# Reordering the vector engine's queue at eleven hand-offs and in the last step of a mixture-of-experts kernel

## The reference

```python
def swiglu(h, wg, wu, wd):
    return (jax.nn.silu(h @ wg) * (h @ wu)) @ wd

def moe_swiglu(h, router, eg, eu, ed):
    b, s, d = h.shape
    t = h.reshape(b * s, d)
    logits = (t @ router).astype(jnp.float32)
    top_v, top_i = lax.top_k(logits, TOP_K)
    top_w = jax.nn.softmax(top_v, axis=-1)
    ...
    out = jnp.zeros((b * s, d), jnp.float32)
    for e in range(N_EXPERTS):
        out = out + combine[:, e:e + 1] * swiglu(t, eg[e], eu[e], ed[e]).astype(jnp.float32)
    return out.astype(h.dtype).reshape(b, s, d)
```

## Time and profile before

| what | value |
|---|---|
| median of 3 runs | 1355.52 us (1355.41 to 1357.62) |
| the profiled execution, its own time | 1355.3 us |
| its span, first to last instruction | 1353.5 us |
| PE busy | 1320.2 us (98%) |
| DVE busy | 1120.3 us (83%) |
| ACT busy | 941.3 us (70%) |
| weight loads in the profile | 423.23 MB on the queue of SP |

### The profile page before, as it was taken

One profiled execution on the slowest core, in us unless ns is written; L12 is line 12 of the kernel. 1 busy time (PEld: TensorE's weight loads), 2 busy tenths in 40 slices (PEclk: granted clock), 3 DMA queues, 4 the chain that ended last, 5 costly groups with the idle time before them and its releaser, 6 DMA issues.

```text
span 1353.5 us, 17501 instructions
## 1 busy us (share of the span) xinstructions
PE 1320.2 (98%) x6684; PEld 1098.8 (81%) x6685; DVE 1120.3 (83%) x1037; ACT 941.3 (70%) x879; POOL 104.2 (8%) x67
## 2 busy tenths in 40 slices
PE   8999999999999999999999999999999999999994
PEld 5898888887898878888888888887888888888873
DVE  5767655556766899999999999999999999999986
ACT  4644444444644778788787887887878787888774
POOL 1140000000231100100001001100000001000020
PEclk9999999999999999999999999999999999999998
DMA  9434655553523799999999999999999999999992
GB/s 354 183 108 161 232 187 186 186 199 113 186 97 138 303 365 378 410 404 420 410 402 421 415 414 403 416 420 375 416 418 404 420 399 410 415 421 419 407 420 92
DMA packets 63029, 437.47 MB, mean 323 GB/s; under 512 B 7231, under 2 KB 7409, under 8 KB 11746
## 3 DMA queue, kind: packets, MB, share of 16 engines
q1 hardware_dynamic: 58896, 423.23, 78.2%
q0 software_dynamic: 3904, 13.06, 2.6%
q10 hardware_dynamic: 146, 0.07, 0.0%
HBM read 430.04 MB, written 6.29 MB: 322 GB/s over the span
## 4 chain that ended last, share of the span: by engine, by line
PE 86%; DVE 8%; ACT 2%; DMA 2%; issue 1%; SPq 0%; DVEq 0%; ACTq 0%
PE ps L2118 34%; PE ps L2142 18%; PE ps L2238 8%; PE ps L1806 4%; DVE w_lo L405 4%; PE ps L2258 4%; PE ps L1821 4%; PE ps L1909 3%; PE ps L2247 2%; PE ps L1783 2%; DMA raw<-in_stream 2%; ACT w_hi L400 1%; PE ps L2134 1%; DVE spare_w L405 1%; PE ps L2178 1%
## 5 line engine op out<-in xcount | busy, mean ns | idle before, releaser
L405 DVE TENSOR_TENSOR w_lo<-raw,w_hi 128x2048 fp32r<-128x2048 f32 x313 | 715.2, 2303 | 125.8 <-ACT w_hi L400 124.8
L400 ACT ACTIVATE w_hi<-raw 128x2048 fp32r<-128x2048 f32 x315 | 600.1, 1917 | 163.6 <-PE ps L2118 67.6
L2118 PE MATMUL ps<-w_hi,xT_hi 128*128 128x512 f32 x564 | 224.3, 398 | 1.8 <-DVE xT_lo L1366 1.3
L2118 PE MATMUL ps<-w_lo,xT_hi 128*128 128x512 f32 x564 | 220.4, 391 | 0.0
L2118 PE MATMUL ps<-w_hi,xT_lo 128*128 128x512 f32 x564 | 219.7, 390 | 0.0
L405 DVE TENSOR_TENSOR spare_w<-raw,spare_w 128x2048 fp32r<-128x2048 f32 x85 | 194.5, 2288 | 10.0 <-ACT spare_w L400 9.5
L400 ACT ACTIVATE spare_w<-raw 128x2048 fp32r<-128x2048 f32 x85 | 163.1, 1918 | 18.7 <-PE ps L2142 16.1
L2118 PEld LDWEIGHTS ps<-w_hi,xT_hi 128*128 128x128 f32 x564 | 106.1, 188 | 23.0 <-DVE xT_lo L1366 1.5
L2118 PEld LDWEIGHTS ps<-w_lo,xT_hi 128*128 128x128 f32 x564 | 105.9, 188 | 22.8
L2118 PEld LDWEIGHTS ps<-w_hi,xT_lo 128*128 128x128 f32 x564 | 106.2, 188 | 20.8
L2142 PE MATMUL ps<-w_hi,aT_hi 128*128 128x512 f32 x288 | 114.1, 396 | 2.6 <-DVE w_lo L405 2.0
(11 more groups left out here) (352 smaller groups left out, 1983.4 us busy)
## 6 DMA issues: line engine op xcount, KB each, us to landing
raw<-in_stream SPq DMA_DIRECT2D x400, 1024.0 KB, 7.9
outs<-work POOLq DMA_DIRECT2D x5, 512.0 KB, 9.2
gain<-in_gains POOLq DMA_DIRECT2D x4, 512.0 KB, 5.3
h<-in_x SPq DMA_DIRECT2D x2, 512.0 KB, 6.7
raw<-in_stream SPq DMA_DIRECT2D x2, 512.0 KB, 6.4
tokens<-big POOLq DMA_DIRECT2D x2, 512.0 KB, 3.3
outs<-work POOLq DMA_DIRECT2D x4, 256.0 KB, 7.6
out<-work SPq DMA_DIRECT2D x4, 256.0 KB, 2.8
```

The source lines that it names most:

```text
L400: nc.scalar.activation(home(n, 0), raw[:, n % RAW, :], ACT.Copy).then_inc(hi_done, 1)
L405: nc.vector.tensor_tensor(home(n, 1), raw[:, n % RAW, :], home(n, 0).bitcast(F32), ALU.subtract).then_inc(lo_done, 1)
L2118: last = nc.tensor.matmul(ps[:, 4 + s, :], (xT_hi, xT_lo)[xp][:, k, x * P:(x + 1) * P], w((n + half), wp, kk * 512, (kk + 1) * 512), start ...
```

## The change

Only DVE's queue is reordered, in its function `step(i)`. Nothing is computed more or less often.

- At the eleven steps of `TURN_AT` the gathered low part stands ahead of `lo_unit(m + 7)` and no longer behind it.
- In step 54 `light_mul` and `light_lo` of the first of the last two light blocks stand ahead of `lo_unit(m + 7)`, the split of the last unit.
- In step 54 `combine(0, 1)` and `combine(1, 1)` go from ahead of `lo_unit(m + 7)` to the very end of the step.

```diff
                 if i == 6:
                     rows()
-                if i == STEPS - 2:
-                    combine(0, 1)
-                    combine(1, 1)
-                lo_unit(dve, m + 7)
                 if i in TURN_AT:
                     p, g = TURN_AT[i]
                     if p < HEAVY:
                         gather_lo_heavy(p, g)
                     else:
                         gather_lo_light(p)
+                if ends:
+                    light_mul(B + 2, 0, 1)
+                    light_lo(B + 2, 0, 1)
+                lo_unit(dve, m + 7)
                 if i in IDS_AT:
                     token_ids(IDS_AT[i])
                 if i == STEPS - 4:
                     last_slots()
-                if ends:
-                    light_mul(B + 2, 0, 1)
-                else:
+                if not ends:
                     lo_unit(dve, m + 8)
                 if ends:
-                    light_lo(B + 2, 0, 1)
                     light_mul(B + 2, 1, 1)
                     light_lo(B + 2, 1, 1)
+                    combine(0, 1)
+                    combine(1, 1)
```

## The result

The changed kernel took 1348.97 us (median of six runs, 1347.65 to 1349.56) against 1355.60 for the kernel before (six runs, 1354.13 to 1357.62): a ratio of 0.9948, 95% interval 0.9936 to 0.9960. The profiled span fell from 1353.5 to 1347.2 us. From L1490 on, a line of the changed kernel has a number one lower than before (L2118 is L2117, L2258 is L2257, L1703 is L1702).

The account below looks back on a forecast made before the run. The weight-load stream was taken to bound the middle, with PE in balance, and DVE's queue the end. From the 1355.52 us median, 4.5 for step 54 and 0 for the hand-offs gave 1351.0 us, range 1350.0 to 1353.9.

Parts of the forecast that it names:

- Step 54: At the end, DVE's reorder starts the result's split (L1703) 4.57 us earlier, taken as 4.5; 3.21 at the low clock.
- The sum: Step 54's moved times added: L1703 at 1335.80 instead of 1340.37, 4.57 us earlier, taken as 4.5.
- The second multiply: Step 54 on DVE: the other light block's multiply at 1332.54, after the last unit's split, its silu ready by 1332.25.
- the `combine` pair: Step 54 on DVE: from 1333.40 to 1335.80, free while PE and ACT need that long, otherwise costing up to 2.40 us.
- ACT's part of the result: After `expert_end` starts at 1333.78, its first half reaches ACT 1.12 us later, at 1334.90.
- ACT's idling ahead of the first `light_hi`: Sign at the end: ACT's idle 5.91 us there should be near 1 us in the new trace.
- Rival 1: At the end, the clock stays low through unit 334: gain only 3.2 us, time 1352.3; chance 0.22.
- The eleven hand-offs: In the middle, gathered low parts moved ahead of splits gain 0; bounds 1.3 us gained and 0.7 lost.
- Rival 4: PE decides in the middle, so its 1.3 us stall comes through as well: 1349.7 us; chance 0.07.
- The bound "1.3 gained": Upper bound for the eleven hand-offs: PE's only wait for such a piece, 1.3 us, gained if PE decides.
- Rival 2: In the middle, late splits at about half the hand-offs pass on 0.68 us each: 4.1 us lost, 1355.1; chance 0.11.
- Rival 3: In the middle, all eleven late splits delay a buffer release: 7.5 us lost against 4.5, 1358.5; chance 0.03.

Follow-up runs that it names:

- run 2: Kernel before with only the eleven hand-offs moved, step 54 as before: 1354.07 us, ratio 0.9988.
- run 3: Kernel before with only step 28's hand-off moved: 1354.53 us, ratio 0.9987.
- run 4: Kernel before with only the ten hand-offs other than step 28's moved: 1355.50 us, ratio 0.9997.
- two half-versions: Kernel before with one half of step 54's reorder each: only the two `combine` calls to the end, 1352.72 us; only the first light block ahead, 1353.44 us.
- run 1: Kernel before with only step 54's reorder, the eleven hand-offs as before: 1350.93 us, ratio 0.9963.
- run 7: Changed kernel with 20 more transposes on PE ahead of step 29's own: 1351.33 us, ratio 0.9960 to the kernel before.
- run 8: Changed kernel with 20 more transposes on PE ahead of step 48's own: 1351.18 us, ratio 0.9967 to the kernel before.
- run 10: Changed kernel once more with no edit: 1348.71 us, ratio 0.9945 to the kernel before.
- run 5: Kernel before with only the two `combine` calls of step 54 moved to the end: 1352.72 us, ratio 0.9971.
- run 6: Kernel before with only the first light block's multiply and low part ahead of the last unit's split: 1353.44 us, ratio 0.9980.
- run 9: Changed kernel with three of the four `combine` calls earlier, each gather having its own semaphore: 1347.21 us, ratio 0.9936 to the kernel before.
- run 11: Changed kernel with three of the four `combine` calls earlier, measured again: 1347.20 us, ratio 0.9937 to the kernel before.

## Why the prediction came out as it did

**Step 54: right, and to the size in the profile.** The sum was 4.57 us, taken as 4.5; the tail shortened by 15.29 - 10.74 = 4.55. Its steps hold one by one, counted from the start of unit 333's split. The second multiply was worked out for 7.46 us behind it and came at 7.48; the `combine` pair for 8.32, came at 8.34; unit 334 done by 8.70, done at 8.62; ACT's part of the result for 9.82, came at 9.77; L1703 for 10.72, L1702 came at 10.74. Run alone the reorder gave 5.0 us by the ratio (3.3 to 6.8 us). One profile of the old order was a slightly flattering measure of it: in the four executions with the old order (before, runs 2, 3 and 4) the tail took 15.29, 15.36, 16.30 and 15.88 us, as `expert_end` behind the gap took 1.98, 2.02, 3.04 and 2.42. Their mean is 15.71, and 15.71 - 10.74 = 4.97 lies close to the 5.0; with an interval of 3.5 us that closeness proves nothing, but the four tails themselves show that 4.55 is at the low end. ACT's idling ahead of the first `light_hi` fell from 5.91 to 2.13 us, not to 1: DVE's queue ends it in any case, and ACT was done with its silu 1325.97 - 1323.38 = 2.59 us into the tail where it had been 1328.49 - 1325.08 = 3.41. That costs nothing.

**Rival 1, a low clock through unit 334: did not come.** The clock was 0.57 and 0.58 from 1326 to 1330, while unit 333 and `fold` ran behind a PE gap of 1.58 us, and 1.00 from 1330 to 1334. In the two half-versions, where a gap of 2.4 or 2.6 us stayed, it was low behind it. The page "TensorE: Matmul & The Clock Gate" of the Trainium skill, section "What's actually happening", says that how many matmuls run slow varies from run to run. The runs show such a variation behind the old order's gap: the same eight matmuls of `expert_end` took 1.98 to 3.04 us, and still 3.04 and 2.42 where the gap was nearly the same (4.78 and 4.80 us in runs 3 and 4). The five tails of the new order agree to 0.01 us (10.74 in the changed kernel, 10.73 in runs 1, 7, 8 and 10), and the absence of a gap is not the whole reason. DVE works through its queue from the split of unit 333 to L1702 and idles only twice for 0.38 us, for ACT's rounding; that sets the tail, and PE and ACT have some 0.2 us to spare. In run 10 the first matmul of unit 334 was still slow, and the eight took 1332.95 - 1330.74 = 2.21 us instead of 1.92; in runs 1 and 7 PE idled for 1.00 us ahead of `expert_end`; the tail was the same. A low clock through the whole unit (3.36 us) would still have cost some 1.2 us, an estimate from 3.36 - 1.92 - 0.2. So the variation was in the old order's figure and hardly in the new one's.

**The eleven hand-offs: the failed step.** "A PE stall in the middle is worth its length only if PE sets the last landing. The loads say no: with three in flight all the time, an earlier PE shortens waits but not the sum of transfers. Value 0". The runs measured 1.6 us for the eleven, 1.8 for step 28 alone, nothing for the other ten, and the length of added PE work when it was added. Rival 4 is what happened. Three loads are in flight because a load is issued as soon as DVE releases a buffer, and DVE follows ACT, which waits for PE. A DMA share of 1.01 says that the engines' queues hold something all the time; it does not say that the stream couldn't run earlier, and it did run earlier or later with PE, by 1.5 to 1.6 and by 2.1 to 2.3 us, at shares of 0.99 to 1.01. The row that tells it was on the table: ACT waited 67.1 us for PE to free a home and 6.1 for landings, so most loads had landed before they were wanted. The prediction read this row rightly ("PE often sets the local order") and then let the number of loads in flight overrule it. The Trainium skill's page "Perfetto Trace Analysis", section "Identifying the Most-Contended Engine", calls the occupancy of 16 DMA engines misleading; the share of 1.01 did mislead here. The prediction's own price for rival 4, 1349.7 us, lay just outside the range that it stated, whose lower end was 1350.0.

The bound "1.3 gained" was a little short too: 1.5 to 1.6 us came through in the traces of equal clock. It was read from the list of waits, which counts from a modelled end; from start to start PE lost 1.90 - 0.35 = 1.55 us at this place, and that is what came through.

**Rivals 2 and 3: no.** The ten other hand-offs have a ratio of 0.9997 [0.9988, 1.0005]. Late splits of 0.68 us each at six or more of them would have cost 4.1 us, 1.0030. The window of 520 to 540 us is unchanged (355 for 356 GB/s).

**What the two profiles overstate.** Of the 6.3 us between the spans, 2.7 are lead at the cast: 1.6 are step 28's, 1.1 the clock's low stretch near 444 us, which the profile of before had and that of after had not. About 1.0 is given back by the split of unit 333, and the tail gives 4.55: 1.6 + 1.1 - 1.0 + 4.55 = 6.25. The traces show where the 1.0 goes. ACT's split of unit 332 waits for its landing in every execution. Before:

```profile
1318.19 1.92 ACT L400 ACTIVATE w_hi<-raw 128x2048 fp32r<-128x2048 f32 x1 [1.58 <-DMA raw<-in_stream]
```

After, it starts at 1316.50, only 1.69 us earlier. The split of unit 333 on DVE follows 6.88 or 6.89 us later in all eleven executions that leave the first two `combine` calls where they were (both kernels, runs 1 to 8 and 10). So in the last 20 us it is the landings that decide, not PE. The window before shows a full DMA there, columns as in the earlier trace rows:

```profile
1310.00:1320.00 10.00, 8.28 (x41) 6.37 (x41) 6.28 (x4) 5.91 (x4) 0.00 (x0) 1.00 1.02 420
```

In the kernel before, units 329 to 332 follow each other on ACT by 3.77 us instead of the 2.6 of the middle, and the four gathers of 0.52 MB for `combine` are on their way at the same time. An estimate with one load and one gather for each such interval, 1.57 MB in 3.77 us, gives 417 GB/s, about the window's 420. From the cast to this split it takes 22.8 to 23.4 us in six executions (the changed kernel, runs 2, 5, 9, 10, 11) and 21.1 to 22.1 in the other seven. In the six POOL had waited 7.7 to 7.9 us for the last write to `outs` before it issued the gathers, in the seven 8.2 to 9.4. Why these differ was not tested, and both groups hold kernels with and without either half of the change.

The medians and ratios, over several executions each, are the better measure of the whole: 5.0 and 1.6 us for the parts, 7.0 for both. The forecast's 4.5 + 0 is short by 1.6 for step 28, which the traces show, and by about 0.5 for the old tail's slower executions. That these come to 2.1 and the median lies 2.0 below the forecast is in part luck, as the intervals are wider than that.

## What to carry to other kernels

Loads always in flight and a DMA share near 1 do not show that the transfers set the pace when each load is issued by the release of a buffer: ask what the first reader of the landed data waits for (here 67 us for PE, 6 for landings), and if in doubt add a piece of known length to the engine that is meant to be free. Ask it for each stage: in the last 20 us of this kernel the landings did decide. An instruction that a busy engine must wait for belongs into the idle time that its producer has ahead of the next piece, and only that one place is worth the move. At an end that is worked off from one queue, put what feeds the next engine first and fill-in work behind it; the times of the old rows, moved and added, gave this part to 0.02 us of one pair of traces, while other executions of the old order differed by up to 1.0 us.

## What was not expected of the hardware

Between 440 and 452 us TensorE's granted clock dropped from the upper level (2.4 GHz) in some executions and not in others, with the same instructions ahead: no stretch in six (the changed kernel, runs 2, 3, 4, 9, 11), one in five (before, runs 1, 5, 8, 10), and nearly twice as long in two (0.79 and 0.64 in runs 6 and 7). PE was busy for 5.58 of the 6 us from 440 to 446 in all of them. One stretch moved everything behind it by about 1.1 us, the long one by 2.6 (1297.6 to 1295.0). It had no pattern by kernel, and the changed kernel's two profiles fell on either side. A comparison of two single profiles to 1 us needs this stretch looked at first.
